# Index scores in head pairs with the forget-gate products dealt between them, and two weight loads' low halves finished by transfers

## The reference

```
def dsa_mix(q, k, v, iq, ik, iw, q_gain, k_gain):
    topk = min(TOPK_MAX, L // 4)                  # 128
    iw32 = iw.astype(f32) * (IDX_HEADS ** -0.5 * IDX_DH ** -0.5)
    ...
        s = jnp.einsum('bqhd,bsd->bqhs', iqb.astype(f32), ik32)
        score = jnp.einsum('bqh,bqhs->bqs', iwb, jax.nn.relu(s))

def hgrn2_mix(q, f_logit, i, g, lb, out_gain):
    z = f_logit.astype(f32)
    ...
    qf = jax.nn.silu(q.astype(f32))
```

## Time and profile before

| | |
|---|---|
| median of 3 executions | 1541.9 us |
| profiled execution | 1541.8 us |
| its span | 1540.0 us |
| TensorE busy | 1521.7 us (99%) |
| VectorE busy | 860.6 us (56%) |
| ScalarE busy | 641.3 us (42%) |
| GpSimd busy | 24.1 us (2%) |

### The profile page before, as it was taken

The page is one execution under the profiler, slowest core; times in us unless marked ns, Lnnn a source line. Parts: engine busy times, 40 slices in busy tenths (PEclk is TensorE's granted clock), DMA queues, the critical chain, the costliest instruction groups (busy, mean ns, idle before and its releaser), DMA issues. The chain is left out here.

```text
span 1540.0 us, 20083 instructions
## 1 busy us (share of the span) xinstructions
PE 1521.7 (99%) x7670; PEld 1268.5 (82%) x7670; DVE 860.6 (56%) x1321; ACT 641.3 (42%) x888; POOL 24.1 (2%) x32
## 2 busy tenths in 40 slices
PE   7999999999999999999999999999999999999999
PEld 7888667888888888888888868999888888888887
DVE  5443565444456877777434778878564543444222
ACT  6442444322245444444333555686653322322210
POOL 0000000000000000000000000010000000000000
PEclk9999999999999999999999999999999999999999
DMA  9313212232233133222333223254312322222232
GB/s 363 132 55 109 103 56 82 83 109 94 98 113 133 55 110 109 83 107 82 137 109 128 69 83 113 56 124 106 91 65 82 110 84 107 87 103 96 95 109 82
DMA packets 25386, 158.33 MB, mean 103 GB/s; under 512 B 2819, under 2 KB 3331, under 8 KB 8300
## 3 DMA queue, kind: packets, MB, share of 16 engines
q1 hardware_dynamic: 23228, 150.01, 27.5%
q0 software_dynamic: 2016, 7.34, 2.5%
q10 hardware_dynamic: 80, 0.13, 0.0%
HBM read 147.87 MB, written 2.13 MB: 97 GB/s over the span
## 5 line engine op out<-in xcount | busy, mean ns | idle before, releaser
L1202 DVE TENSOR_TENSOR w_lo<-raw,w_hi 128x2048 fp32r<-128x2048 f32 x109 | 249.8, 2292 | 347.3 <-ACT w_hi L644 347.2
L1952 PE MATMUL bank<-h_hi,w_hi 128*128 128x512 f32 x1096 | 431.5, 394 | 1.1 <-DVE cy L1544 0.8
L1954 PE MATMUL bank<-h_hi,w_lo 128*128 128x512 f32 x1096 | 427.0, 390 | 0.0
L1953 PE MATMUL bank<-h_lo,w_hi 128*128 128x512 f32 x1096 | 426.7, 389 | 0.0
L644 ACT ACTIVATE w_hi<-raw 128x2048 fp32r<-128x2048 f32 x123 | 235.0, 1910 | 321.7 <-PE bank L1954 307.4
L1952 PEld LDWEIGHTS bank<-h_hi,w_hi 128*128 128x128 f32 x1096 | 205.6, 188 | 45.3 <-issue 2.8
L1954 PEld LDWEIGHTS bank<-h_hi,w_lo 128*128 128x128 f32 x1096 | 205.3, 187 | 43.7
L1953 PEld LDWEIGHTS bank<-h_lo,w_hi 128*128 128x128 f32 x1096 | 205.5, 188 | 42.0 <-issue 0.2
L1952 PE MATMUL bank<-a_hi,w_hi 128*128 128x512 f32 x352 | 136.9, 389 | 0.0
L1953 PE MATMUL bank<-a_lo,w_hi 128*128 128x512 f32 x352 | 136.9, 389 | 0.0
L1954 PE MATMUL bank<-a_hi,w_lo 128*128 128x512 f32 x352 | 136.9, 389 | 0.0
(11 more groups left out here) (315 smaller groups left out, 2005.2 us busy)
## 6 DMA issues: line engine op xcount, KB each, us to landing
raw<-weights SPq DMA_DIRECT2D x128, 1024.0 KB, 4.8
w_lo<-raw POOLq DMA_DIRECT2D x14, 512.0 KB, 5.0
toep<-bias_scratch SPq DMA_DIRECT2D x8, 448.0 KB, 4.6
x<-xT SPq DMA_DIRECT2D x2, 1024.0 KB, 12.7
x_tok<-x_tok SPq DMA_DIRECT2D x1, 2048.0 KB, 13.8
mem2T<-mem2T SPq DMA_DIRECT2D x2, 1024.0 KB, 5.3
outT<-x SPq DMA_DIRECT2D x8, 256.0 KB, 4.2
lead<-lead SPq DMA_DIRECT2D x2, 512.0 KB, 4.7
```

Of the source, the lines that this page charges most:

```text
L1202: nc.vector.tensor_tensor(w_lo[PLACE[m]][:, :], raw[m % 2][:, :], w_hi[PLACE[m]][:, :].bitcast(F32), ALU.subtract).then_inc(lo_ready, 1)
L1952: nc.tensor.matmul(o, lh, rh, start=first, stop=False)
L1953: nc.tensor.matmul(o, lh, rl, start=False, stop=False)
L1954: return nc.tensor.matmul(o, ll, rh, start=False, stop=last)
```

## The change

- The index scores are computed in pairs, two heads at a time, over 64 rows each; there is one key tile `ik` now with the key in both halves, and GpSimd's two clears of it are gone. Behind each of the 12 pairs stand two products (six matmuls) of the three remaining forget-gate tiles. `turn_km` comes behind all of that and goes to banks 4 and 5 instead of 2 and 3.
- ScalarE rounds the second `hf` load before the index weights and scores instead of behind them, rounds `hq`'s first load behind score 13 (counted from 0) and subtracts its two parts behind scores 14 and 15.
- VectorE does other work between pairs of accumulations (`between_scores`): the second `hf` load's split in two parts, three of the four normalizations, the first mask and the first three rounds of the top keys. Rounds 3 to 9 stand behind the split of the second `hq` load.
- The low halves of the first `hq` load and of `sk` are made by ScalarE and GpSimd's transfers. `BY_DMA` has 12 loads now, no longer in one row, and `low_done` gives the semaphore to wait for.

```diff
 LEVEL_PRODUCTS = (32, 46, 60, 74, 88, 102, 115, 128)
-BY_DMA = range(FIRST["mq"], FIRST["w_out_2"] + 1)
+BY_DMA = [FIRST["hq"], *range(FIRST["sk"], FIRST["w_out_2"] + 1)]
...
+    tiles("turn_km", 2, (4, 5))
     tiles("hf", 4, first=FIRST["hf"], per=2)
...
+
+        def low_done(m):
+
+            if m in BY_DMA:
+                return lo_added, 32 * (BY_DMA.index(m) + 1)
+            return lo_ready, m + 1 - sum(b < m for b in BY_DMA)

...
+            def add_lows(first, last):
+
+                for n_ in range(first, last):
+                    m = BY_DMA[n_]
+                    if n_:
+                        pool.wait_ge(lo_added, 32 * n_)
+                    for part in range(2):
+                        cut = slice(part * SLOT // 2, (part + 1) * SLOT // 2)
+                        pool.wait_ge(minus_hi, 2 * n_ + part + 1)
+                        nc.gpsimd.dma_start(w_lo[PLACE[m]][:, cut], raw[m % 2][:, cut], accum_op=ALU.add
+                                            ).then_inc(lo_added, 16)
+
...
-            nc.scalar.dma_start(ik[1][64:P, :], ik[0][0:64, :]).then_inc(ik_odd_in, 16)
+            nc.scalar.dma_start(ik[64:P, :], ik[0:64, :]).then_inc(ik_odd_in, 16)
             head_root(MT * SAH)
+            round_w(FIRST["hf"] + 1)
             ready(("iw", 0))
...
                 frees(("idx", w), nc.scalar.activation(relu[w % 2][:, 0:keys], B(("idx", w))[:, 0:keys], ACT.Relu))
+                if w == 13:
+                    round_w(FIRST["hq"])
+                if w in (14, 15):
+                    minus_part(FIRST["hq"], w - 14)

...
             for m in range(2):
-                round_w(FIRST["hf"] + m + 2)
+                if m:
+                    round_w(FIRST["hq"] + 1)
                 for t in (2 * m, 2 * m + 1):
...
             for m in range(2):
                 round_w(FIRST["hq"] + m + 2)
+                for part in range(2) if m else ():
+                    minus_part(FIRST["sk"], part)
                 for t in (2 * m, 2 * m + 1):
...
             dve.wait_ge(set_up, 3)
             dve.wait_ge(mask_in, 32)
             wait_free(("iw", 0))
...
+            def hide_later(i):
+
+                cut = sel[:, i, P * i:P * (i + 1)]
+                link(nc.vector.tensor_tensor(cut, cut, causal[:, :], ALU.add))
+
+            def between_scores(pair_):
+
+                if pair_ in (1, 2):
+                    split_part(FIRST["hf"] + 1, pair_ - 1)
+                if pair_ in (3, 5, 9):
+                    t = {3: 0, 5: 1, 9: 2}[pair_]
+                    ready(("hf", t))
+                    normal("hf", t, lf[:, t * S:(t + 1) * S])
+                if pair_ == 4:
+                    dve.wait_ge(relu_used, IDXH + 2)
+                    hide_later(1)
+                if pair_ in (6, 10, 11):
+                    r = {6: 0, 10: 1, 11: 2}[pair_]
+                    top_keys(r, r + 1)
+
...
-                if m == 0:
-                    split_w(FIRST["hf"] + 1)
-                for t in (2 * m, 2 * m + 1):
-                    ready(("hf", t))
-                    normal("hf", t, lf[:, t * S:(t + 1) * S])
-                split_w(FIRST["hf"] + m + 2)
-                top_keys(5 * m, 5 * m + 5)
+            for i in (2, 3):
+                hide_later(i)
+            ready(("hf", 3))
+            normal("hf", 3, lf[:, 3 * S:4 * S])
+            split_w(FIRST["hq"] + 1)
+            top_keys(3, 10)
...
                     ready(("hq", t))
                     normal("hq", t, qf[:, t * S:(t + 1) * S])
-                split_w(FIRST["hq"] + m + 2)
+                if m == 0:
+                    split_w(FIRST["sq"])
                 top_keys(10 + 5 * m, 15 + 5 * m)

...
-                claim(("idx", w_))
-
-                done(("idx", w_), nc.tensor.matmul(B(("idx", w_))[:, 0:P * (i + 1)], iq[:, h // 2, i * P:(i + 1) * P],
-                                                   ik[h % 2][:, 0:P * (i + 1)], start=True, stop=True))
+            for w_ in range(0, len(IDX), 2):
+                for e in range(2):
+                    claim(("idx", w_ + e))
+                for e in range(2):
+                    i, h = IDX[w_ + e]
+                    rows_ = slice(64 * e, 64 * e + 64)
+                    done(("idx", w_ + e), nc.tensor.matmul(
+                        B(("idx", w_ + e))[:, 0:P * (i + 1)], iq[rows_, h // 2, i * P:(i + 1) * P],
+                        ik[rows_, 0:P * (i + 1)], start=True, stop=True))
+                for p_ in (KT + w_, KT + w_ + 1):
+                    t, kt = divmod(p_, KT)
+                    ld, key, cs = FIRST["hf"] + t // 2, ("hf", t), slice(t % 2 * P, (t % 2 + 1) * P)
+                    if kt == 0:
+                        weights(ld)
+                        claim(key)
+                    ins = product(B(key)[:, :], w(ld, 1)[:, kt, cs], w(ld, 0)[:, kt, cs], h_hi[:, kt, :], h_lo[:, kt, :],
+                                  kt == 0, kt == KT - 1)
+                    if kt == KT - 1:
+                        done(key, ins)
             turn_heads("turn_km", km_tok, M)
```

More of the change, by code:

```diff
@@ L373, in build @@
         v_hg = at("v_hg", AR + 32 * K, [TT, S])
[L374 removed]
+        ik = at("ik", AR + 40 * K, [S])
         relu = [at(f"relu{s}", AR + (44 + 2 * s) * K, [S]) for s in range(2)]
@@ L568, in _ @@
             stream(FIRST["idx"] + 1, BY_DMA[0] + 2)
-            for n_, m in enumerate(BY_DMA):
-                sp.wait_ge(lo_added, 32 * (n_ + 1))
+            for m in range(BY_DMA[0], BY_DMA[-1] + 1):
+                sp.wait_ge(*low_done(m))
                 load(m + 2)
@@ L611, in _ @@
             pool.wait_ge(padded, 4)
-            for n_, m in enumerate(BY_DMA):
-                if n_:
-                    pool.wait_ge(lo_added, 32 * n_)
-                for part in range(2):
-                    cut = slice(part * SLOT // 2, (part + 1) * SLOT // 2)
-                    pool.wait_ge(minus_hi, 2 * n_ + part + 1)
-                    nc.gpsimd.dma_start(w_lo[PLACE[m]][:, cut], raw[m % 2][:, cut], accum_op=ALU.add
-                                        ).then_inc(lo_added, 16)
+            add_lows(1, len(BY_DMA))
         @block.scalar
@@ L1702, in _ @@
             wait_free(("iw", 0))
-            for w, (i, h) in enumerate(IDX):
-                keys = P * (i + 1)
-                wait_free(("idx", w))
-                if w:
-                    dve.wait_ge(relu_used, w)
-                nc.vector.scalar_tensor_tensor(out=sel[:, i, 0:keys], in0=relu[w % 2][:, 0:keys],
-                                               scalar=iw[:, i, h:h + 1], in1=sel[:, i, 0:keys], op0=ALU.mult,
-                                               op1=ALU.add).then_inc(relu_used, 1)
-            dve.wait_ge(relu_used, len(IDX))
-            for i in range(1, TT):
-                link(nc.vector.tensor_tensor(sel[:, i, P * i:P * (i + 1)], sel[:, i, P * i:P * (i + 1)], causal[:, :],
-                                             ALU.add))
             def top_keys(first, last):
```

38 lines of the change are left out of this document (16 added, 22 removed).

## The result

The changed kernel took 1544.37 us (median of 19 executions, 1543.25 to 1545.78), the kernel before on the same chips 1541.98 us (19 executions, 1541.49 to 1543.03). The ratio is 1.0015, with a 95% interval of 1.0009 to 1.0020. The forecast was 1542.0 with a range up to 1543.5; the result is 0.9 us above the range. The profiled execution took 1544.8 us, its span is 1543.0: 3.0 us more than before, the medians differ by 2.4. It is one of the slower of the 19. Their mean granted clocks differ too: 14 had 0.999 and took 1543.25 to 1544.90 (median 1543.9), five had 0.998 or 0.997 and took 1544.37 to 1545.78. What the profile shows is therefore good to about half a microsecond as a measure of the median.

A forecast was written before the change was run, and what follows sets the result against it. TensorE was taken to bound the kernel, its 3.4 us lead spent in a wait of about 3.8 us at the fourth query tile, 0.2 lost: 1541.8 + 0.2 = 1542.0 us, range 1540.2 to 1543.5.

The forecast's parts named there:

- What bounds the kernel: Whole kernel: TensorE bounds it, busy for 1521.7 us of 1540.0; in the index stretch the clock takes no part.
- the row at 962.05: Fourth query tile: TensorE idles 0.31 us for the first tile's bank, which ScalarE copies out at 961.52; called the most important row.
- Part 1: Index scores: head pairs with products between take 12.6 us instead of 15.66, saving TensorE 3.1 us; 3.4 us ahead at the turn.
- the wait at the second tile: Second forget-gate tile: TensorE waits 0.16 us for its bank, as ScalarE's rounding now stands ahead of the index weights' copy.
- Part 2: First query load: its transferred low half lands by 927.1, against the need at 927.8; takes 2.2 us from VectorE.
- Rival (b): First query load's low half lands late, making the kernel slower: 1543.5 at 3 us late; chance 0.07.
- (c): Rival: the relay through two relu buffers loses more per pair, 0.3 us more giving 1543.8; chance 0.07.
- (d): Rival: the two heads' matmuls don't run beside each other, the turn comes 5.5 us later, time 1547.5; chance 0.02.
- What is late next: Fourth query tile: TensorE arrives at 958.3, waits about 3.8 us for ScalarE's copy; the 3.4 us lead goes, 0.2 lost.
- chain of 34 us: VectorE and ScalarE work from the memory keys' turn at 927.85 to the copy at 961.7, starting the fourth tile at 962.25.
- the later stages ... keep their distance: Behind the fourth query tile: later stages, fed by TensorE's turns, keep their distance to it.
- (a): Rival: the gain survives, with the 3.4 us lead and 0.3 of the wait remaining, 1538.1; chance in full 0.06.

The follow-up runs named there:

- the last experiment: The best version with one matmul per head over 128 rows again instead of pairs, products still dealt between: 1542.30 us, ratio 1.0002 to the kernel before.
- the pairs alone: The kernel before with the scores in head pairs, nothing dealt between them and no added transfers: 1542.61 us, ratio 1.0004.
- The filled wait: The changed kernel with 16 extra matmuls, whose output nobody reads, ahead of the fourth query tile: 1542.02 us, ratio 1.0001 to the kernel before.
- the wait forced on the kernel before: The kernel before, its fourth query tile made to wait for VectorE's first level result: 1546.58 us, ratio 1.0030.
- The best version: The changed kernel with the fourth query tile in bank 3 and top-key rounds 18 and 19 moved behind the levels: 1539.28 us, ratio 0.9982 to the kernel before.
- the two kernels whose waits were filled: Changed kernel with 16 extra matmuls ahead of the fourth query tile, 1542.02 us; with that tile in bank 3 and 6 before the first level, 1539.90 us.

## Why the prediction was wrong

- **What bounds the kernel**: right as to TensorE and the row at 962.05, incomplete in one sentence, "so the clock takes no part". It was said of the index stretch, where it is true (1.00 there after the change too); the question was never asked again at the place where the forecast put a wait of 3.8 us.
- **Part 1**: right. The 12 pairs with two products each ran at the forecast lengths (2.22 against 2.21 us at 256 keys), the wait at the second tile was 0.32 us where 0.16 was said (the copy's own rows, 896.70 + 0.74 + 1.9, give 899.34 and not 899.15, and so 0.35), the first query product came at 927.71 (927.8). That pairing is worth 3 us of the end is shown by the last experiment, and that it needs the products between by the one with the pairs alone.
- **Part 2**: right. GpSimd issued the two halves at 917.5 and 918.6, against a forecast of 918.6 and half a microsecond, and they landed in 4.8 to 6.3 us, by 925, ahead of the need at 927.7. Rival (b) did not happen. Nor did (c) and (d).
- **What is late next**: the step that failed. Its chain of 34 us was right to 0.1 us (955.12 against 955.2, 961.61 against 961.7, 962.14 against 962.25), and so was the wait (3.64 against 3.8). The failure is in the sentence that closes it, "the 3.4 us lead is gone with 0.2 lost": a wait was priced at its own length. The runs put a second term beside it, 2.3 us in the profiled execution, because TensorE's clock was at 1.2 GHz from within the wait until 5.4 us after it. The filled wait shows it from one side (the tile no earlier, but 2.98 us long instead of 5.28), the wait forced on the kernel before from the other (3.1 us late, 4.5 us slower).
- **A smaller miss**: "the later stages ... keep their distance". A transferred low half came 0.5 us later relative to TensorE at 1013.65. With the 16 matmuls in the wait that wait is absent, so its size hangs on small shifts; no experiment isolated it.
- **Rivals**: the 1.8 us of idle VectorE ahead of the split, on which (a) and (c) count, were 1.96 us in the profile (930.50 to 932.46). They are slack for a late VectorE, as (c) uses them; for a late TensorE they are none, as the last experiment shows. The chance of (a) in full is 0.06 in the list and 0.07 in the sentence on being faster; nothing rests on the difference.
- **The range** took in late transfers and the relay, both above the forecast and both absent, and had no term for what a wait does to the work behind it. Add 2.3 to the forecast and it is 1544.3; 1544.37 was measured. That they agree so closely is in part luck: the 2.3 come from one execution, most of the others had less of the low clock, and the later low half was not in the forecast either.
- **Where the expected gain went**: TensorE's 3.4 us were all spent in the wait for bank 0. They were real: with the bank changed and the next wait of VectorE shortened, 2.6 of them reach the end.

## What to carry to other kernels

When a change makes the bounding engine arrive early at something that isn't ready, price the wait twice: its own length, which only takes back the gain, and what the idle time does to TensorE's clock afterwards, which can make the kernel slower than before. The granted clock in narrow windows behind each wait of more than a microsecond, and the mean clock of each timed execution, show it; the 40 slices of the page did not. Before the gain is given up, look at what the wait is for: here it was one bank number and the place of two rounds of the top keys.

## What the runs showed of the hardware

- The clock's fall doesn't follow the wait alone. It came 2.2 us into a wait of 3.6 us, and 1.30 and 1.10 us after work had resumed behind waits of 3.3 and 3.6 us. In two of the three cases TensorE was at work again when the clock fell. The stretches at 1.2 GHz were 6.83, 3.42 and 6.83 us long.
- The three kernels with a wait of 3.3 to 3.6 us in their profile had a mean clock below 1.000 in all of their 31 executions. Of those whose profile shows a shorter one, part had it: 6 of 11 with 1.41 us, 3 of 11 with 1.79, 6 of 11 with 1.98, 4 of 11 with 2.36. All four profiles are of executions that kept the clock, so how long the wait was in the others is not shown. Such a kernel has two times, 1.2 to 3 us apart, and its median says little.
- The best version and its variant without pairs, whose longest waits between 890 and 1110 us are 1.3 and 1.1 us, kept 1.000 in all 22 executions, and so did the kernel before, with 1.1 us, in the 99 that were timed beside these. The pairs alone, with ten waits of up to 0.73 us close together and one of 1.1, had 0.999 in 2 of 11, whose times do not stand apart.
- Matmuls whose output nobody reads kept the clock up in 22 of 22 executions of the two kernels whose waits were filled.
